# Unread products in TensorE's waits behind each norm and in the delta rule's chunk loop

## The reference, cut to what matters

```python
def layer_norm(x, g, b):
    mu = jnp.mean(xf, -1, keepdims=True)
    var = jnp.mean(jnp.square(xf - mu), -1, keepdims=True)
    return (xf - mu) * lax.rsqrt(var + LN_EPS) * g + b

def adaln_sublayer(x, m, f, ln_g, ln_b):          # six of these: 4 ffn, hybrid, mla
    shift, scale, gate = m[:, None, 0], m[:, None, 1], m[:, None, 2]
    y = f(x * (1 + scale) + shift)
    return layer_norm(DEEPNORM_ALPHA * x + (1 + gate) * y, ln_g, ln_b)

def rmsnorm(x, g):                                # in front of the two layers of the second block
    return x * lax.rsqrt(jnp.mean(x * x, -1, keepdims=True) + RMS_EPS) * g

def gated_delta_rule(q, k, v, g, beta):           # 4 heads, 4 chunks of 64 tokens
    ...
    def step(state, xs):
        q_i, k_i, u_i, w_i, g_i, a_i = xs
        v_new = u_i - w_i @ state
        o = (q_i * jnp.exp(g_i)[..., None]) @ state + a_i @ v_new
        k_dec = k_i * jnp.exp(g_last[..., None] - g_i)[..., None]
        state = state * jnp.exp(g_last)[..., None, None] + jnp.einsum('bhcd,bhce->bhde', k_dec, v_new)
        return state, o
    _, o = lax.scan(step, s0, (qc, kc, u, w, gc, attn_intra))
```

## Time and profile before

| | |
|---|---|
| median of 3 executions | 1860.48 us (1859.42 to 1862.66) |
| the profiled execution, its own time | 1859.86 us |
| its span in the profile | 1858.1 us |
| TensorE matmul busy | 1593.3 us, 86% |
| VectorE busy | 1060.5 us, 57% |
| ScalarE busy | 830.3 us, 45% |
| mean granted TensorE clock | 0.922 |

### The profile page before, as it was taken

One profiled execution on the slowest core, in us unless ns is written; L12 is line 12 of the kernel. 1 busy time (PEld: TensorE's weight loads), 2 busy tenths in 40 slices (PEclk: granted clock), 3 DMA queues, 4 the chain that ended last, 5 costly groups with the idle time before them and its releaser, 6 DMA issues.

```text
span 1858.1 us, 29314 instructions
## 1 busy us (share of the span) xinstructions
PE 1593.3 (86%) x12073; PEld 1510.2 (81%) x12073; DVE 1060.5 (57%) x1894; ACT 830.3 (45%) x1442; POOL 0.2 (0%) x4
## 2 busy tenths in 40 slices
PE   2999979947777999979999668879997898779887
PEld 2999969935766999969999566779996797679856
DVE  5877757673634777757773545455453544444463
ACT  1434443317144444344433456454342884355463
POOL 0000000000000000000000000000000000000000
PEclk9999989878858999989999879989998999989998
DMA  9878829400002878828883050245552451435100
GB/s 364 318 278 304 289 84 347 154 23 1 1 23 69 306 270 302 292 81 300 302 288 107 23 170 30 91 137 182 185 179 68 137 179 38 136 93 182 46 2 23
DMA packets 195537, 297.42 MB, mean 160 GB/s; under 512 B 11122, under 2 KB 159692, under 8 KB 195404
## 3 DMA queue, kind: packets, MB, share of 16 engines
q1 hardware_dynamic: 192576, 293.07, 46.2%
q10 hardware_dynamic: 2828, 2.48, 0.4%
HBM read 294.47 MB, written 1.05 MB: 159 GB/s over the span
## 4 chain that ended last, share of the span: by engine, by line
PEld 47%; PE 32%; DVE 8%; ACT 6%; issue 3%; DVEq 1%; ACTq 1%; PEldq 1%
PEld bank L542 16%; PEld bank L540 15%; PEld bank L541 14%; PE bank L540 6%; PE bank L541 6%; PE bank L542 6%; PE bank L1022 3%; PE bank L1009 2%; PE bank L1039 2%; PEld bank L360 1%; PE bank L494 1%; DVE uT L350 1%; ACT arena L1074 1%; DVEq L487 1%; PE bank L2131 1%
## 5 line engine op out<-in xcount | busy, mean ns | idle before, releaser
L540 PE MATMUL bank<-u_hi,w_hi 128*128 128x256 f32 x1408 | 403.5, 287 | 34.2 <-DVE w_lo L645 31.2
L541 PE MATMUL bank<-u_lo,w_hi 128*128 128x256 f32 x1408 | 402.3, 286 | 0.0
L542 PE MATMUL bank<-u_hi,w_lo 128*128 128x256 f32 x1408 | 402.0, 286 | 0.0
L645 DVE TENSOR_TENSOR w_lo<-weight_ring,w_hi 128x1024 fp32r<-128x1024 f32 x264 | 307.9, 1220 | 17.1 <-ACT w_hi L613 16.7
L540 PE MATMUL bank<-src_hi,wp_hi 128*128 128x256 f32 x880 | 264.7, 301 | 49.4 <-DVE wp_lo L823 49.4
L540 PEld LDWEIGHTS bank<-u_hi,w_hi 128*128 128x128 f32 x1408 | 274.3, 195 | 36.2 <-issue 35.1
L541 PEld LDWEIGHTS bank<-u_lo,w_hi 128*128 128x128 f32 x1408 | 274.5, 195 | 0.0
L542 PEld LDWEIGHTS bank<-u_hi,w_lo 128*128 128x128 f32 x1408 | 274.3, 195 | 0.0
L613 ACT CAST w_hi<-weight_ring 128x1024 fp32r<-128x1024 f32 x264 | 260.6, 1045 | 22.4 <-PE bank L542 16.9
L541 PE MATMUL bank<-src_lo,wp_hi 128*128 128x256 f32 x880 | 258.1, 293 | 0.0
L542 PE MATMUL bank<-src_hi,wp_lo 128*128 128x256 f32 x880 | 257.6, 293 | 0.0
(11 more groups left out here) (342 smaller groups left out, 2448.8 us busy)
## 6 DMA issues: line engine op xcount, KB each, us to landing
weight_ring<-in_mod_w_dram SPq DMA_DIRECT2D x72, 1024.0 KB, 7.0
weight_ring<-in_ffn_w_gate_dram SPq DMA_DIRECT2D x44, 1024.0 KB, 5.9
weight_ring<-in_ffn_w_up_dram SPq DMA_DIRECT2D x44, 1024.0 KB, 5.5
weight_ring<-in_ffn_w_down_dram SPq DMA_DIRECT2D x44, 1024.0 KB, 8.4
weight_ring<-in_hyb_w_in_dram SPq DMA_DIRECT2D x16, 1024.0 KB, 7.8
weight_ring<-in_w_in_e_dram SPq DMA_DIRECT2D x16, 1024.0 KB, 5.4
weight_ring<-in_w_in_o_dram SPq DMA_DIRECT2D x13, 1024.0 KB, 5.4
weight_ring<-in_hyb_w_out_dram SPq DMA_DIRECT2D x4, 1024.0 KB, 4.9
```

The lines of the kernel that those rows point to most:

```text
L540: nc.tensor.matmul(out, lhs[0], rhs[0], start=start, stop=False, skip_group_check=group)
L541: nc.tensor.matmul(out, lhs[0], rhs[1], start=False, stop=False, skip_group_check=group)
L542: return nc.tensor.matmul(out, lhs[1], rhs[0], start=False, stop=stop, skip_group_check=group)
L645: nc.vector.tensor_tensor(part_view(wl, n, part), raw, part_view(wh, n, part).bitcast(F32), ALU.subtract).then_inc(w_lo.sem, w_lo.up())
```

## The change

A helper `keep_warm(bank, n, width)` issues n float32 products of `ones` with the first `width` columns of the tables in SBUF into a bank that nobody reads. They wait for nothing and raise nothing. They stand in four places:

- `residual_norm`: 16 of 256 columns into bank 6, behind the sum of the squares and ahead of TensorE's drain (six times);
- `rms_features`: 14 of 256 columns into bank 6, behind the sum of the squares (twice);
- `ws`: one of 128 columns into bank 4g+3, ahead of the wait (six times in all);
- `state_out`: two of 128 columns into bank 4g+3, ahead of the wait (eight times in all).

The outputs of both heads of a group go into bank 4g+2 now, the second head's into its columns 64 to 127; bank 4g+3 takes no outputs any more.

```diff
+        def keep_warm(bank, n, width=SEQ):
+
+            for _ in range(n):
+                nc.tensor.matmul(bank[:, 0:width], ones[:, :], tab[:, 0:width], start=True, stop=True)
...
                 last.then_inc(sum_done.sem, sum_done.up())
+                keep_warm(PB[6], 16)
                 pe.drain().then_inc(stage_done.sem, stage_done.up())
...
                         def ws(pe):
+                            keep_warm(PB[4 * g + 3], 1, P)
                             pe.wait_ge(gstep[g].sem, gstep[g].count)
...
                     def state_out(pe):
+                        keep_warm(PB[4 * g + 3], 2, P)
                         pe.wait_ge(gstep[g].sem, gstep[g].count)
...
-                            o = PB[4 * g + 2 + h][:, 0:CHUNK]
+                            o = PB[4 * g + 2][:, h * CHUNK:(h + 1) * CHUNK]
...
-                            ins = nc.scalar.copy(wide(kbe, g)[:, h, t - CHUNK:t], PB[4 * g + 2 + h][:, 0:CHUNK])
+                            ins = nc.scalar.copy(wide(kbe, g)[:, h, t - CHUNK:t], PB[4 * g + 2][:, h * CHUNK:(h + 1) * CHUNK])
...
                 last.then_inc(step_done.sem, step_done.up())
+                keep_warm(PB[6], 14)
```

## The result

The changed kernel takes **1866.35 us**, median of 7 executions (1865.09 to 1867.42), against 1860.48 for the kernel before (7 executions, 1858.85 to 1862.66). The ratio is 1.0032, with a 95% interval of 1.002 to 1.0043: some 6 us slower, where 8 us faster was forecast. It lies outside the range given (1846 to 1864).

A forecast was written before the change was run, and what follows sets the result against it. TensorE was taken to set the time, losing some to waits and the low clock. Terms -4.5 - 0.7 + 1.0 - 3.9 = -8.1 us gave 1851.8 for the profiled execution, 1852.4 us for the median, range 1846 to 1864.

The forecast's parts named there:

- The chunk loop: Delta rule's chunk loop: six fillers per chunk hold the high clock for shorter chunks and faster sums behind, -3.9 us.
- the filler's price: In the chunk loop: a 128-column product takes 0.22 us at the high clock, 0.44 at the low one.
- a chunk of 6.2 us at the high clock: Chunk loop: 5.3 us plus 0.9 for fillers, some 0.4 of their 1.3 us falling into TensorE's waits.
- My break-even of 0.9 chunks: Chunk loop: dearer than before once more than 0.9 of its three chunks is at the low clock.
- The norms: Norms 1 to 5: fillers shorten TensorE's wait from 10.3 to 3.1 us, giving less low clock at restarts, -4.5 us.
- the 3.0 us of low clock: Restarts behind norms 1 to 5: low clock assumed after the 3.1 us wait, taking 2.8 us of it off.
- Last norm and first rms_features: There: sum of squares gains 1.1 us, TensorE's drain is 0.8 late, restart gains 0.4; together -0.7 us.
- Second rms_features: There: fillers end 2.1 us late, shorter low clock at the restart returns 1.1; together +1.0 us.
- The shared bank: Chunk loop outputs: sharing one bank costs nothing, as the two copies and the `o_taken` wait stay as before.
- the second rival's loop: Chunk loop if fillers don't hold the clock: chunks 2 and 3 take 11.3 us each, +6.0 us; chance 0.11.
- The chance of 0.11 for slower: Whole kernel: probability given to a time over 1864.2 us, against 0.62 for faster and 0.27 for same.

The follow-up runs named there:

- e6: Changed kernel without norm and rms_features fillers, loop fillers doubled to two ahead of ws and four ahead of state_out; one execution, 1865.72 us.
- e2: Changed kernel with only the sixteen fillers behind residual norms, no loop or rms_features fillers; 1859.07 us, ratio 0.9989.
- e4: Kernel before with both heads' outputs in one shared bank and no filler anywhere; 1860.74 us, ratio 0.9999.
- e8: Changed kernel with only the norms' sixteen fillers, plus six at the head of TensorE's part in ffn and projection stages; 1843.55 us, ratio 0.99.
- e11: Changed kernel without loop fillers and shared bank: sixteen behind residual norms, fourteen behind rms_features; 1861.39 us, ratio 1.0009.
- e3: Changed kernel with only the fourteen fillers in the two rms_features, no norm or loop fillers; 1867.12 us, ratio 1.0034.
- e5: Changed kernel without norm and rms_features fillers, loop cut to one filler ahead of group 1's ws and one ahead of group 0's state_out; 1865.1 us, ratio 1.002.

## Why the prediction was wrong

**The chunk loop, forecast -3.9: wrong, and the step that failed is the filler's price inside it.** I took 0.22 us each, from products that follow their like the earlier trace rows, let 0.4 us of them fall into TensorE's waits, and came to a chunk of 6.2 us at the high clock. It takes 7.47. A chunk was to grow by 0.9 us and grew by 2.2. Put between half-array and 64-column products, each place costs some 0.20 more (e6), and of the 0.4 hardly anything is absorbed. Chunk 0 and three chunks at 7.47 are 3.25 + 22.4 = 25.7 us even with the high clock throughout, against 25.8 before (from the first `state_out` at 511.63 to the end of the loop at 537.4): there was nothing to win. With chunk 3 at 12.9 the loop is +5.2. Behind the loop 2.5 us come back, where the changed kernel has less low clock, and ahead of it 0.2 are lost; the stage is left with +2.9. That the clock would hold longer was right (it fell 10.4 us later), as was the point that chunks at the low clock cost most: forecast 11.3, measured 12.9. My break-even of 0.9 chunks at the low clock is in truth none.

**The norms, forecast -4.5: right in kind, half in size.** The fillers' time, the unchanged start of ScalarE and the wait (forecast 3.1, measured 3.49) came as said. The step that failed is the 3.0 us of low clock taken for a wait of that length. The rows show 6.0, 6.5, 5.7, 0.0 and 3.4, mean 4.3. At the restarts the products are +0.1, +0.3, +0.2, -2.0 and -0.5 us against before: -1.9 together. e2 alone measured -2.2. And a gain at a restart isn't yet one at the stage's end: the mla stage starts 2.0 us ahead and ends 1.1 late. Its waits in attention are where the clock falls next, one of 12.3 us ahead of L930 and one of 3.5 ahead of the output projection, before and after alike. Windows of before, then of the changed kernel:

```profile
1113.80:1124.00 10.20, 2.89 (x14) 2.76 (x15) 6.69 (x19) 1.22 (x3) 0.00 (x0) 0.50 0.46 166
1175.30:1178.70 3.40, 3.40 (x18) 3.40 (x18) 3.40 (x5) 3.40 (x5) 0.00 (x0) 0.50 0.38 96
```

```profile
1113.80:1127.70 13.90, 5.75 (x28) 5.49 (x29) 7.39 (x24) 3.27 (x6) 0.00 (x0) 0.51 0.43 150
1175.40:1182.20 6.80, 5.10 (x24) 5.13 (x25) 6.62 (x9) 6.63 (x9) 0.00 (x0) 0.50 0.42 130
```

Both stretches are longer by about 3.4 us. I had counted no such handing back.

**Last norm and first rms_features, forecast -0.7: measured -0.4** (+0.29 and -0.66). That it is so near is luck. The sum of squares was to gain 1.1 us and gained 0.2: the clock fell right ahead of it (low from 1438.2 to 1441.7), 2.1 us behind the fillers. The restart was to gain 0.4 and gained 1.1, of which the even layer kept 0.7. The drain was late by 0.5 instead of 0.8.

**Second rms_features, forecast +1.0: right at its place, wrong at the end.** The drain is late by 1.77 (forecast 2.1) and the restart gives back 0.8 (1.1). But the odd layer takes 1.1 us more, not 0.8 less: its low stretches are longer here too. The first of them has no wait ahead of it: in the kernel before TensorE is busy throughout with 64 products of 30 columns (L2444, 1674.85 to 1683.26) as the clock falls at 1680.4. Like the loop, it shows the clock falling in busy time. Windows of before and of the changed kernel:

```profile
1680.40:1687.20 6.80, 6.80 (x33) 6.80 (x34) 1.13 (x1) 0.00 (x0) 0.00 (x0) 0.50 0.83 246
```

```profile
1684.00:1694.20 10.20, 10.20 (x49) 10.20 (x49) 2.12 (x2) 0.00 (x0) 0.00 (x0) 0.50 0.76 217
```

**The shared bank, forecast 0:** right (e4).

So the size came near the second rival's loop (+6.0), though not by its way: there the chunks were to be slow at the low clock, here three of four are slow at the high one. (The rival's loop counts 0.2 us twice: 6.2 + 11.3 + 11.3 is 28.8, so +5.8.) Of the 14.6 us between forecast (-8.1) and measurement (+6.5) the loop makes 6.8, handing back in mla and odd layer 5.0 (1.1 + 2.0, and 1.1 + 0.8), the norms' restarts 2.6; small things make the rest. The chance of 0.11 for slower was too small because the filler's price in the loop had one bound only, though the range of the unknown costs should have had two.

The Trainium skill ("TensorE: Matmul & The Clock Gate", Part 1, "HAM oscillation") puts the fall of the clock down to TensorE standing idle. For the norms e8 agrees: with the wait down to 0.58 us no restart was low. In the loop the fall came with TensorE busy 5.70 of 5.70 us, yet the advice of the Trainium skill would have been the better guide: it gives no reason for work where there is no wait.

**What stays open:** why one and the same wait of 3.49 us leaves the clock high or low, and why stages that start high (mla in e2, e11 and the change) get longer low stretches in attention while in e8 mla keeps its 2.0 us. Behind the hybrid stage it is no scatter: mla is +1.0 in e2 and e11 and +1.1 in the change, the odd layer +1.1 in e3, e11 and the change. Ahead of the loop it may be, with 4.3 us between executions of the same instructions. It wasn't tried to move attention's waits by themselves.

## What to carry to other kernels

Fillers pay where they cover a wait to its last microsecond without being late: the half cover gave 2 us, the full one 17.7. Inside a dense loop they are work like any other, and here cost more than their length (0.42 us for one instead of 0.22) between products of another shape; measure one at its place before counting on it. A gain of clock is to be read at the end of the stage, not at the restart.

## What the runs showed of the hardware

- At the high clock a lone 128-column float32 filler costs 0.42 us between half-array products, two 0.64, four 1.08: 0.20 once and 0.22 for each. That the 0.20 belongs to the change of shape is read from rows and not tested.
- TensorE's clock fell with the engine busy all the time in two places of the kernel before: in the chunk loop (5.70 of 5.70 us), and in the 30-column products of the odd layer (5.50 of 5.50 us up to the fall at 1680.4). With twice the fillers (e6) it stayed at 1.00 through the whole loop.
- At the low clock, in e5, one filler costs 0.73 us (523.74 to 524.47 below), and chunks with two of them take 10.6 (525.51 to 536.10) instead of 8.9:

```profile
523.74 0.80 PE L448 MATMUL bank<-tables_sb,ones 128*128 128x128 f32 x2
524.47 1.12 PE L1778 MATMUL bank<-arena 128*64 128x128 f32 x4
525.51 0.80 PE L448 MATMUL bank<-tables_sb,ones 128*128 128x128 f32 x2
...
536.10 0.80 PE L448 MATMUL bank<-tables_sb,ones 128*128 128x128 f32 x2
```

- More time at the high clock isn't less time: the changed kernel has 58 us less at 0.50 than before and is slower; e11 and the changed kernel both have 232 us at 0.50, and lie 4 us apart, each against its own runs of before (ratios 1.0009 and 1.0032).
